# Modulation computed in pieces inside other stages, and block experts with the tokens as the stationary operand

## The reference, cut to what matters

```python
sh1, sc1, g1, sh2, sc2, g2 = jnp.split((jax.nn.silu(c) @ ada_w + ada_b)[:, None, :], N_MOD, axis=-1)
hl = rmsnorm(xl, norm1_g) * (1 + sc1) + sh1
...
xl = xl + g1 * (jnp.concatenate([a_l, b_l, cv_l], axis=-1) @ w_o)
xl = xl + g2 * ec_ffn(rmsnorm(xl, norm2_g) * (1 + sc2) + sh2, router_w, w_gate, w_up, w_down)
...
def expert_block(args):          # second block: 128 tokens of one expert
    xb, e = args
    g, u = jnp.split(xb @ w_up[e], 2, axis=-1)
    return (jax.nn.silu(g) * u) @ w_down[e]
```

## Time and profile before

| | us |
|---|---|
| median of 3 runs | 5797.83 |
| lowest and highest | 5785.93, 5798.45 |
| the profiled execution | 5791.35 |
| its span | 5789.7 |

### The profile page before, as it was taken

How to read it: one execution, slowest core, us unless ns; L and a number is a source line. 1 busy time by engine, 2 the same in 40 slices (tenths; PEclk the granted TensorE clock), 3 DMA queues, 4 the chain that set the end, 5 groups by cost and what they waited for, 6 DMA issues and landing times. The chain is left out here.

```text
span 5789.7 us, 66936 instructions
## 1 busy us (share of the span) xinstructions
PE 4554.2 (79%) x25106; PEld 3155.3 (54%) x25106; DVE 2171.4 (38%) x4322; ACT 1061.3 (18%) x2073; POOL 509.5 (9%) x588
## 2 busy tenths in 40 slices
PE   6997876938998589797756984799776667699993
PEld 1674554426776066455335860477555444587773
DVE  0223544163433222455145431111476633344444
ACT  0112333020111021234110100111254301000111
POOL 0010001201111001000200101100110100100001
PEclk9998988958999799999868997899998777899997
DMA  7312011007774631201207967601102300788884
GB/s 259 92 43 55 19 25 54 23 37 241 228 243 140 237 96 46 66 2 25 65 30 272 335 225 212 217 34 38 57 26 71 139 33 32 281 322 312 323 321 160
DMA packets 392043, 786.84 MB, mean 136 GB/s; under 512 B 104116, under 2 KB 171276, under 8 KB 390572
## 3 DMA queue, kind: packets, MB, share of 16 engines
q1 hardware_dynamic: 334424, 676.64, 33.6%
q0 software_dynamic: 19232, 62.98, 4.0%
q10 hardware_dynamic: 38144, 43.91, 2.5%
HBM read 655.30 MB, written 128.16 MB: 135 GB/s over the span
## 5 line engine op out<-in xcount | busy, mean ns | idle before, releaser
L2784 PE MATMUL bexp_gu<-bexp_xT,bexp_wu 128*128 128x128 f32 x4096 | 477.5, 276 | 25.8 <-DVE bexp_ex L2810 12.7
L2784 PEld LDWEIGHTS bexp_gu<-bexp_xT,bexp_wu 128*128 128x128 f32 x4096 | 469.2, 193 | 46.4 <-issue 27.1
L2769 PE MATMUL bexp_acc<-bexp_wd,bexp_hid 128*128 128x512 f32 x512 | 225.1, 592 | 2.9 <-DVE bexp_hid L2816 2.9
L508 PE MATMUL p_ring<-p_hT,p_wc 128*128 128x256 f32 x1008 | 221.4, 383 | 3.1 <-DMA p_wc<-in_w_in 3.1
L508 PEld LDWEIGHTS p_ring<-p_hT,p_wc 128*128 128x128 f32 x1008 | 193.0, 192 | 30.2 <-issue 3.5
L159 PE MATMUL m_acc<-m_wt,m_sl 128*2 128x512 f32 x192 | 92.8, 641 | 121.6 <-DMA m_wt<-in_w_mod 119.6
L1580 PE MATMUL l0exp_acc<-l0exp_wd,l0exp_hid 128*32 128x512 f32 (+1 forms) x512 | 171.2, 597 | 2.6 <-DVE l0exp_hid L1622 2.6
L516 PE MATMUL p_ring<-p_wt,p_hT 128*128 128x400 f32 (+2 forms) x480 | 170.8, 516 | 0.0
L1563 PE MATMUL l0exp_gu<-l0exp_xT,l0exp_wg 128*128 128x160 f32 x1024 | 166.5, 320 | 4.5 <-DVE l0exp_xT L1607 4.5
L2810 DVE TENSOR_SCALAR bexp_ex<-bexp_ex 128x128 f32<-128x128 f32 x128 | 28.7, 224 | 371.7 <-ACT bexp_ex L2741 371.7
L1563 PEld LDWEIGHTS l0exp_gu<-l0exp_xT,l0exp_wg 128*128 128x128 f32 x1024 | 154.8, 204 | 17.8 <-issue 12.6
(11 more groups left out here) (608 smaller groups left out, 8344.7 us busy)
## 6 DMA issues: line engine op xcount, KB each, us to landing
bexp_wu<-in_w_expert_up SPq DMA_DIRECT2D x32, 4096.0 KB, 14.1
bexp_wd<-in_w_expert_down SPq DMA_DIRECT2D x32, 2048.0 KB, 10.0
l0exp_wg<-in_exp_w_gate SPq DMA_DIRECT2D x16, 2048.0 KB, 8.9
l0exp_wu<-in_exp_w_up SPq DMA_DIRECT2D x16, 2048.0 KB, 14.0
l0exp_wd<-in_exp_w_down SPq DMA_DIRECT2D x16, 2048.0 KB, 10.6
l1exp_wg<-in_exp_w_gate SPq DMA_DIRECT2D x16, 2048.0 KB, 9.5
l1exp_wu<-in_exp_w_up SPq DMA_DIRECT2D x16, 2048.0 KB, 14.6
l1exp_wd<-in_exp_w_down SPq DMA_DIRECT2D x16, 2048.0 KB, 13.3
```

Source lines behind the costliest of these rows:

```text
L508: mm = nc.tensor.matmul(out[:, i * PC:(i + 1) * PC], wc[:, k, b * 128:(b + 1) * 128], hT[ch % 2][:, k, :], start=(k == 0), stop=(k == KD - 1))
L2769: mm = nc.tensor.matmul(acc[2 * j + c][:, :], hid[j][:, f, :], wd[j][:, f, c * 512:(c + 1) * 512], start=(f == 0), stop=(f == KF - 1))
L2784: mm = nc.tensor.matmul(gu[f % 2][:, h, :], wu[j][:, k, h * FF + f * 128:h * FF + (f + 1) * 128], xT[j][:, k, :], start=(k == 0), stop=(k ...
```

## The change

The stage `modulation` is gone. A class `Modulating` computes the six column groups of 1024 columns (4 MB each) in pieces inside other stages, into `cols` and `gates` of their own for each layer. Groups 0 to 2 of layer 0 are made in `setup`, its groups 3 to 5 in `mix_out` of layer 0 (one weight buffer, products after the tiles 4, 6 and 8), and all six of the following layer in each latent `route_choice` (three weight buffers; loads issued by ACT, products after the tile loop and before PE's last transposes). A group is 32 products of 128x2 by 128x256, four at a time into the partitions 0, 32, 64 and 96 of one PSUM bank. ACT copies out, PE turns the columns, POOL adds biases and makes `cols`, SP stores the gates. The zeros of F are stored by SP in `route_choice`, which also puts its two small PSUM tiles into one bank.

The neighbourhood bias is made by POOL alone, behind its own work in `diff_attention`, and POOL issues all its DMAs. Each head's gather, add and store follow one another.

`block_experts` makes the tokens the stationary operand for gate and up: per block 16 products of 128x128 by 128x512 (32 instructions) for both halves. DVE and ACT work on 512 columns at once, the hidden activations come out with the token on the partitions, PE turns them (4 transposes) and ACT copies them back. PE's order is gate, turn of the hidden block before, up, turn of the next tokens, down product of the block before.

```diff
--- before.py
+++ after.py
...
-def modulation(nc, name, c, c_ctx, w, b, gain1, gain2, cols, gates, identity, beside=None):
...
+class Modulating:
...
+        self.wt = [st.sb(f"{tag}wt{j}", [128, KD, D]) for j in range(bufs)]
...
+    def load_small(self, eng):
+        parts = [self.gain1, self.gain2] + [self.b[g * D:(g + 1) * D] for g in (0, 1, 3, 4)]
+        for i, src in enumerate(parts):
+            eng.dma_start(self.small[i * KD:(i + 1) * KD, :], src.rearrange("(k p) -> k p", p=128)).then_inc(self.small_in, 16)
...
+    def load(self, eng, n):
+        if n >= self.bufs:
+            eng.wait_ge(self.multiplied, START + n - self.bufs + 1)
+        g = self.groups[n]
+        eng.dma_start(self.wt[n % self.bufs][:, :, :], self.w[:, g * D:(g + 1) * D].rearrange("(k p) n -> p k n", p=128)).then_inc(self.w_in[n % self.bufs], 16)
+
...
+    def products(self, pe, n):
+        pe.wait_ge(self.w_in[n % self.bufs], START + 16 * (n // self.bufs + 1))
+        if n:
+            pe.wait_ge(self.evicted, START + 4 * n)
+        for k in range(KD):
+            for q in range(4):
+                mm = self.nc.tensor.matmul(self.acc[32 * q:32 * q + 2, 0:256], self.silu[:, k, :], self.wt[n % self.bufs][:, k, q * 256:(q + 1) * 256],
+                                           start=(k == 0), stop=(k == KD - 1))
+        mm.then_inc(self.multiplied, 1)
+
+    def evict(self, act, n):
+        act.wait_ge(self.multiplied, START + n + 1)
...
+        for q in range(4):
+            self.nc.scalar.activation(self.rows[n % 2][:, q * 256:(q + 1) * 256], self.acc[32 * q:32 * q + 2, 0:256], ACT.Copy).then_inc(self.evicted, 1)
+
+    def turn(self, pe, n):
+        if self.is_gate(n):
+            return
+        pe.wait_ge(self.evicted, START + 4 * (n + 1))
+        pe.wait_ge(self.small_taken, START + 1)
+        pe.wait_ge(self.col_taken, START + self.cols_to(n))
+        for k in range(KD):
+            tp = self.nc.tensor.transpose(self.turned[:, 64 + 2 * k:66 + 2 * k], self.rows[n % 2][:, k * 128:(k + 1) * 128], self.identity[0:2, 0:2])
+        tp.then_inc(self.row_turned, 1)
+
...
+    def wait_end(self, eng):
+        eng.wait_ge(self.col_made, START + self.cols_to(len(self.groups)))
+        if self.gates_to(len(self.groups)):
+            eng.wait_ge(self.row_stored, START + 16 * self.gates_to(len(self.groups)))
...
+def setup(nc, X, identity, x, ctx, vectors, silus, modulate):
...
+                for i, src in enumerate(vectors):
+                    sp.dma_start(raw[i * KD:(i + 1) * KD, :], src.rearrange("(k p) -> k p", p=128)).then_inc(vec_in, 16)
+                mod.load_small(sp)
+                for n in range(N):
+                    mod.load(sp, n)
                 sp.dma_start(X[:, 0:CTX_TILES, :], ctx.rearrange("(t p) n -> p t n", p=128)).then_inc(loaded, 16)
...
+                pe.wait_ge(steps, START + 4)
+                for n in range(N):
+                    mod.products(pe, n)
+                    mod.turn(pe, n)
...
+        def after(g):
+            return len(tiles) - 1 - 2 * (N - 1 - g)
...
+                if mod:
+                    act.wait_ge(w_in, START + w_total[0])
+                    for n in range(mod.bufs):
+                        mod.load(act, n)
...
+                    if mod and n == after(0):
+                        mod.take_small(act)
+                    for g in range(N):
+                        if n == after(g):
+                            mod.evict(act, g)
+                            if g + mod.bufs < N:
+                                mod.load(act, g + mod.bufs)
+                            mod.take(act, g)
...
+                    if mod and n + 1 == after(0):
+                        mod.turn_small(pe)
+                    for g in range(N):
+                        if n + 1 == after(g):
+                            mod.products(pe, g)
+                            mod.turn(pe, g)
...
-def route_choice(nc, name, first, count, X, cols_a, cols_b, col, router_w, XN, cap, choice_idx, choice_aff, identity):
+def route_choice(nc, name, first, count, X, cols_a, cols_b, col, router_w, XN, cap, choice_idx, choice_aff, identity, zero=None, modulate=None):
...
+                if zero is not None:
+                    sp.wait_ge(zeroed, START + 1)
+                    for t in tiles:
+                        sp.dma_start(F[t * 128:(t + 1) * 128, :], zeros[:, :]).then_inc(sums_zeroed, 16)
...
+                if mod:
+                    for n in range(mod.bufs):
+                        mod.load(act, n)
...
+                if mod:
+                    mod.take_small(act)
+                    for n in range(N):
+                        mod.evict(act, n)
+                        if n + mod.bufs < N:
+                            mod.load(act, n + mod.bufs)
+                        mod.take(act, n)
...
+                        pe.wait_ge(aff_taken[j], START + i)
...
+                if mod:
+                    mod.turn_small(pe)
+                    for n in range(N):
+                        mod.products(pe, n)
+                        mod.turn(pe, n)
...
+                        modulate=(lambda st: modulate(st, 0, [3, 4, 5], 1)) if l == 0 else None)
...
+            route_choice(nc, n + "route", CTX_TILES, LAT_TILES, X, a2, b2, 0, t["router_w"][l], XN, 128, lat_idx, lat_aff, identity,
+                         (F, range(0 if both else CTX_TILES, TILES)), lambda st: modulate(st, l + 1, list(range(6)), 3))
...
+    def on_gpsimd(po):
+        po.dma_start(mk[:, :], mask).then_inc(mask_in, 16)
+        nc.gpsimd.memset(rep[:, :, :, :], 0.0).then_inc(zeroed, 1)
+        po.wait_ge(zeroed, 1)
         for h in range(N_HEADS):
             inner = rep[:, h, 2:2 + 2 * N_ROWS - 1, 48:48 + 2 * N_COLS - 1]
+            po.dma_start(inner, rpb[h].partition_broadcast(GRID)).then_inc(cleared, 16)
+        po.wait_ge(cleared, 16 * N_HEADS)
+        for h in range(N_HEADS):
+            inner = rep[:, h, 2:2 + 2 * N_ROWS - 1, 48:48 + 2 * N_COLS - 1]
+            nc.gpsimd.tensor_scalar(inner, inner, N_DK ** 0.5, None, ALU.mult).then_inc(scaled, 1)
+        po.wait_ge(scaled, N_HEADS)
+        po.dma_start(padded.rearrange("q h r c -> q (h r c)"), rep[:, :, :, :].rearrange("q h r c -> q (h r c)")).then_inc(placed, 16)
+        po.wait_ge(placed, 16)
+        po.wait_ge(mask_in, 16)
         for h in range(N_HEADS):
             if h >= 2:
+                po.wait_ge(bias_stored[h - 2], 16)
             for pat in range(PATTERNS):
                 for a in range(2):
                     src = dram_view(padded.tensor, h * 19 * 127 + (9 - 2 * pat - a) * 127 + 63, [[W - 1, 64], [127, 10], [1, 64]])
                     dst = bt[h % 2][64 * a:64 * a + 64, pat * BAND:(pat + 1) * BAND].rearrange("p (r c) -> p r c", c=GRID)
+                    po.dma_start(dst, src).then_inc(bias_in[h], 16)
+            po.wait_ge(bias_in[h], 160)
+            nc.gpsimd.tensor_tensor(bt[h % 2][:, :], bt[h % 2][:, :], mk[:, :], ALU.add).then_inc(added, 1)
+            po.wait_ge(added, h + 1)
+            po.dma_start(BT[h], bt[h % 2][:, :]).then_inc(bias_stored[h], 16)
         for h in range(N_HEADS):
+            po.wait_ge(bias_stored[h], 16)
+    return on_gpsimd
...
+                def take(i, j):
+                    act.wait_ge(hid_turned[j], START + i + 1)
+                    act.wait_ge(downed[j], START + i * 2)
+                    nc.scalar.activation(hid[j][:, :, :], hidP[:, :, :], ACT.Copy).then_inc(hid_taken[j], 1)
...
+                    act.wait_ge(gate_done[j], START + i + 1)
+                    if not first:
+                        act.wait_ge(steps[1 - j], START + (i + j) * 4)
+                    nc.scalar.activation(ex[:, :], gu[0][:, :], ACT.Exp, scale=-1.0).then_inc(raised[j], 1)
+                    if not first:
+                        take(i + j - 1, 1 - j)
+                        write(i + j - 1, 1 - j)
                     if last:
+                        take(i, j)
                         write(i, j)
...
+                def hid_turn(i, j):
+                    pe.wait_ge(steps[j], START + (i + 1) * 4)
+                    for f in range(KF):
+                        tp = nc.tensor.transpose(hidP[:, f, :], hidR[j][:, f * 128:(f + 1) * 128], identity[:, :])
+                    tp.then_inc(hid_turned[j], 1)
...
                     pe.wait_ge(up_in[j], START + (i + 1) * 16)
-                    for f in range(KF):
-                        if f >= 2:
-                            pe.wait_ge(steps[j], START + (i * KF + f - 1) * 4)
-                        elif not first:
-                            pe.wait_ge(steps[1 - j], START + ((i + j) * KF + f - 1) * 4)
-                        for h in range(2):
-                            for k in range(KD):
-                                mm = nc.tensor.matmul(gu[f % 2][:, h, :], wu[j][:, k, h * FF + f * 128:h * FF + (f + 1) * 128], xT[j][:, k, :],
-                                                      start=(k == 0), stop=(k == KD - 1))
```

(38 more changed lines are left out.)

401 lines of the change are left out of this document (200 added, 201 removed).

## The result

The changed kernel takes **5458.65 us** (median of four runs, 5451.89 to 5462.22) against 5798.14 for the kernel before: a ratio of **0.9417, 95% interval 0.9406 to 0.9428**. The profiled execution has a span of 5450.2 us where the one before has 5789.7, so the two traces differ by 339.5 us, like the medians.

What follows compares the result with a forecast made beforehand. The kernel's time was taken as the sum of its barrier-ended stages, PE bounding block experts. -396 + 41 + 16 + 4 + 52 - 27 = -310 gave span 5480, profiled 5481, plus 4: 5485 us; own range 5440 to 5530, full 5435 to 5615.

Steps and rivals of the forecast that it cites:

- The removed stages: Three modulation stages disappear: 402.8 us less an estimated 2 us at each border, counted as -396.
- The products' price: A modulation group's 64 PE instructions on four column strips run side by side: 4.2 us, against 13.7 in series.
- rival 2: Modulation products: column strips do not overlap; +12 in setup, +29, +33 twice, giving 5592 us; chance 0.14.
- Setup: Setup stage: twelve small DMAs, weights and X loaded, gate store behind X; 58 us instead of 17, +41.
- l0out: Layer 0's mix_out stage: PE is the bound, so three groups' products, evictions and turns add +16 (45 in series).
- Route stages: Two route stages: three ACT loads ahead of the squares cost +1.5 us, with more semaphores +2 each; the rest is covered.
- The bias: Diff attention: POOL's serial chain of 161 us against 109 of cover, at 2.0 us a DMA issue: +52.
- rival 1: Diff attention's bias: POOL issues slowly, 3.3 to 5.1 us a DMA, +150 to 176: 5585 to 5610; chance 0.2.
- Block experts: Block experts stage: a block takes 22.15 us instead of 23.0, over 32 blocks -27, bounds -33 and 0.
- rival 3: Block experts gain nothing because weights land after the block's end: 5512 us; chance 0.05.
- The unchanged stages: The other 22 stages, none changed, were forecast to differ by 0.
- Rival 4: Diff attention: DVE stops POOL's DMA writing, 8.9 us for 40 DMAs, +276 on the 52; slower than before; chance 0.03.

Runs made afterwards that it cites:

- Experiment 8: Changed kernel with the four quarters of a setup modulation product sent to the same two PE output partitions, in four banks: 5476.78 us (one run).
- Experiment 3: Changed kernel with only two weight loads ahead of ACT's squares in the route stages, the third behind its tile loop: 5445.19 us.
- experiment 4: Changed kernel with the route stages' first two weight loads behind ACT's squares and root, the third behind its tile loop: 5433.32 us.
- the faster versions: Changed kernel with later route loads and paired bias gathers, add in ten pieces: 5427.28 us; with the bias also spread over POOL's idle time: 5424.72, add whole 5424.5.
- experiment 1: Changed kernel with the block experts put back to the form of the kernel before: 5484.66 us, ratio 0.9464.
- few bytes: Changed kernel whose expert blocks, after two whole experts, load only 128 rows each of up and down weights, all instructions kept: 5473.9 us (one run).
- the seven kernels: The changed kernel and six variants of it with the bias gathers, POOL's add or the bias's place altered: 5424.5 to 5470.76 us.
- experiment 7: Changed kernel with two route loads ahead of the squares, bias gathers of two heads back to back, POOL's add in five pieces: 5437.23 us.

## Why the prediction was right, and where it was not

The time is 26 us under the forecast of 5485, within its own range, and none of the rivals came true. The largest terms, the removed stages, the hidden work and the experts, were right by their mechanism. That no more than 26 us are missing is in part luck: 20 us more than forecast, 15 of them in the route stages, stand against 50 less (bias, unchanged stages, setup). Point by point:

- **The removed stages** (-396): -395.6, right, with the 2 us taken off at each border.
- **The products' price** (4.2 us a group): right in its mechanism and a little high, 3.63 at the full clock, 5.0 to 5.3 in setup. The guess for eviction and turn (2 us) was 1.70 and 0.65. Experiment 8 settles rival 2: in series it is 13.97.
- **Setup** (+41): +36.2. Two steps were off. SP's twelve small DMAs, taken at 0.57 us each, took 4.1 us in all, not 7. And the gate's store, +3 behind X, cost nothing: it was issued at 48.90, and X landed at 52.4. The 46 us from the first weight load to X's landing are as reckoned, so the stage is set by its 17.8 MB.
- **l0out** (+16): +18.2. Right: PE's work, not hidden.
- **Route stages** (+2 each): **+9.3 each, the largest miss in proportion.** The step that failed is "ACT issues three loads ahead of the squares: +1.5 us". The price of an issue was right for the first two, 0.4 to 0.6 us, and not for the third, 8.2 to 8.4. Experiment 3 shows that it is the third; experiment 4 that the whole growth goes once the loads come later. A second cost stood behind the first: the small load issued after 8 MB. The steps on the cover (70 us for the loads, PE's groups under the top-k) were right, with 17 us to spare.
- **The bias** (+52): +26.9. Mechanism right, two terms of a head mis-sized, in opposite directions and by different amounts, and one missed. An issue of 640 pieces took 0.74 us (0.717 to 0.777), far under my 2.0 and below my lower bound of 1.4: 7.2 us a head instead of 20. So rival 1 was far off. (Its lower end was also added up wrongly: by the same chain 3.3 us a DMA give +104, not +150.) The wait for landing was 4.2 us for the first head and 8.3 to 8.6 for the other three, where I had 2. The first head took 19.1 us and the others 23.4 to 24.4, not 30. And the cover, which I took as fixed at 109 us, moved: the attention became 12.3 us longer. I had seen POOL and DVE stop each other in the earlier trace rows and counted nothing for it, "the chain is later than that anyway". For the changed kernel that was correct, since the bias ended last. It is what remained in the faster versions.
- **Block experts** (-27): -23.8 in the stage, 25.5 between experiment 1 and the changed kernel. Period 21.9 and 22.3 to 22.6, forecast 22.15, and 21.9 with few bytes, which is what PE's instructions had been added up to. The loads cost 7.0 us, so "thin but enough" was right, and rival 3 was not.
- **The unchanged stages** (0): -20.0. This is the second reason, beside the bias, that the forecast was high. It goes with PE's granted clock. Window attention of layer 0 (l0swa), before and after, has the same 1074 instructions of PE, 3.6 us less busy time and a higher clock (columns as above):

```profile
784.00:971.10 187.10, 145.20 (x1074) 104.96 (x1074) 99.59 (x300) 86.62 (x241) 13.46 (x34) 0.93 0.09 20
```
```profile
699.50:882.80 183.30, 141.62 (x1074) 102.45 (x1074) 99.66 (x300) 86.61 (x241) 13.53 (x34) 0.95 0.08 20
```

By the clocks of their windows, the 22 unchanged stages ran 806 us at the lower of the two levels before and 762.5 after. The 43.5 us between are worth up to 22 us, as an estimate, since at the lower level PE does half its work. The prediction took the clock of these stages as unchanged, and it wasn't. What lets it fall differently in stages with the same code stays open.
- **Rival 4**, that POOL's writing of DMAs is stopped by DVE, did not happen: 30 of the 40 issues ran beside an operation of DVE, and the longest took 0.777 us. The Trainium skill (SBUF — State Buffer, the two sides of SBUF and who interferes with whom) says that a DVE operation in a two-port mode starves descriptors written by GpSimd, and gives 620 against 3100 ns; the prediction had applied this to any DVE work. No such stretch shows here. What the same page says of operations is what this case shows: the skill says that an operation of DVE with two SBUF inputs and one of GpSimd that reads SBUF take a shared port pair as an exclusive lock, for the whole instruction. By it a DVE operation that meets an add ends one operation's length after the add, and the rows agree (POOL until 4018.48, DVE until 4019.83; 4041.99 and 4043.35). They agree less with the page's rule that the one that starts first gets the pair: of nine operations of DVE's line that had started ahead of an add in the seven kernels, five, 0.56 to 0.99 us ahead, went through unheld or nearly so, and four, 0.08 to 1.35 us ahead, were held; the one that led by 1.35, in experiment 7, for four pieces.

The sum by terms: bias -25, unchanged stages -20, setup -5 against routes +15, experts +3, l0out +2, which is the -29.5 between -310 and -339.5.

## What to carry to other kernels

A large load can hold the engine that issues it: ahead of work that everything waits for, issue no more of them than the trace shows to pass at 0.4 to 0.6 us, put small loads that are needed soon ahead of large ones even on another queue, and never queue a store that frees a buffer behind them. When work is hidden beside an engine, ask also what it does to that engine's own operations: the cover is not a fixed number. Where a serial chain of gather, wait, add and store waits for landings, issue the next gather first. And before a difference of a few us in a stage is put down to an edit, compare PE's granted clock over it.
